# First block's attention as one chain of 16 heads, woven with sections and output projection; modulation and context products placed elsewhere

## The reference

```python
for i in range(DEPTH):                        # 2 layers
    h = rms_norm(x, ln_attn_g[i])
    dq, dk, dv, mq, mk, mv = jnp.split(h @ w_in[i], cuts, axis=-1)   # six sections of 512 columns
    y_diff = diff_attention(...)              # 8 score maps in 4 pairs, a = p0 - lam * p1, value width 128, rms_norm
    y_moba = moba_attention(...)              # 8 heads of 64, causal, 256 keys
    x = x + jnp.concatenate([y_diff, y_moba], axis=-1) @ w_out[i]
    x = x + conv_ffn(rms_norm(x, ln_ffn_g[i]), w_up[i], conv_w[i], conv_b[i], w_down[i])
```

## Time and profile before

| | us |
|---|---|
| median of 3 runs | 2213.57 (2211.42 to 2217.89) |
| the profiled execution: time | 2213.08 |
| its span, first to last instruction | 2211.3 |
| PE busy | 2112.7 (96%) |
| DVE busy | 1361.5 (62%) |
| ACT busy | 961.3 (43%) |
| POOL busy | 206.2 (9%) |

### The profile page before, as it was taken

One profiled execution on the slowest core, in us unless ns is written; L12 is line 12 of the kernel. 1 busy time (PEld: TensorE's weight loads), 2 busy tenths in 40 slices (PEclk: granted clock), 3 DMA queues, 4 the chain that ended last, 5 costly groups with the idle time before them and its releaser, 6 DMA issues.

```text
span 2211.3 us, 31532 instructions
## 1 busy us (share of the span) xinstructions
PE 2112.7 (96%) x12146; PEld 1816.3 (82%) x12146; DVE 1361.5 (62%) x2350; ACT 961.3 (43%) x1602; POOL 206.2 (9%) x173
## 2 busy tenths in 40 slices
PE   7889999989999999998999999999999999999998
PEld 5668998767999888887888778888877899888997
DVE  5646676674777525738454554877565578475565
ACT  4444555544555525344332363223244564445443
POOL 1420000141000100000010000111011000100100
PEclk9979999988999999999999999999999999999999
DMA  9434655522555422212132103534324234251543
GB/s 249 143 123 173 240 182 177 195 95 73 185 191 182 160 100 77 70 57 67 58 105 90 63 20 103 214 132 145 105 89 155 86 115 135 98 178 58 187 157 124
DMA packets 79068, 285.01 MB, mean 129 GB/s; under 512 B 8823, under 2 KB 9731, under 8 KB 78921
## 3 DMA queue, kind: packets, MB, share of 16 engines
q1 hardware_dynamic: 70560, 256.15, 34.4%
q10 hardware_dynamic: 6072, 18.73, 2.3%
q0 software_dynamic: 2288, 8.13, 1.4%
HBM read 277.14 MB, written 5.83 MB: 128 GB/s over the span
## 4 chain that ended last, share of the span: by engine, by line
PE 69%; DVE 8%; ACT 4%; issue 2%; POOL 0%; DVEq 0%; ACTq 0%
PE pb L923 13%; PE pb L925 13%; PE pb L924 13%; PE pb L935 5%; PE pb L937 5%; PE pb L936 5%; PE pb L941 2%; PE pb L1154 2%; PE pb L1257 2%; PE pb L1238 1%; DVE SPL L1916 1%; ACT SPH L1378 1%; PE pb L1082 1%; PE pb L1081 1%; PE pb L1080 1%
## 5 line engine op out<-in xcount | busy, mean ns | idle before, releaser
L1916 DVE TENSOR_TENSOR SPL<-RAW,SPH 128x1024 fp32r<-128x1024 f32 x433 | 524.2, 1229 | 412.9 <-ACT SPH L1378 397.4
L923 PE MATMUL pb<-HTH,SPH 128*128 128x256 f32 (+1 forms) x2008 | 649.8, 324 | 7.9 <-POOL HTL L2518 2.8
L925 PE MATMUL pb<-HTH,SPL 128*128 128x256 f32 (+1 forms) x2008 | 639.7, 319 | 0.0
L924 PE MATMUL pb<-HTL,SPH 128*128 128x256 f32 (+1 forms) x2008 | 639.5, 318 | 0.0
L1378 ACT ACTIVATE SPH<-RAW 128x1024 fp32r<-128x1024 f32 x462 | 475.0, 1047 | 272.6 <-PE pb L925 118.6
L923 PEld LDWEIGHTS pb<-HTH,SPH 128*128 128x128 f32 x2008 | 384.2, 191 | 41.0 <-issue 6.5
L924 PEld LDWEIGHTS pb<-HTL,SPH 128*128 128x128 f32 x2008 | 384.6, 192 | 26.2
L925 PEld LDWEIGHTS pb<-HTH,SPL 128*128 128x128 f32 x2008 | 384.3, 191 | 26.2
L935 PE MATMUL pb<-SPH,HTH 128*128 128x512 f32 x544 | 219.1, 403 | 16.8 <-DVE SPL L1916 6.3
L936 PE MATMUL pb<-SPH,HTL 128*128 128x512 f32 x544 | 214.9, 395 | 0.0
L937 PE MATMUL pb<-SPL,HTH 128*128 128x512 f32 x544 | 214.7, 395 | 0.0
(11 more groups left out here) (275 smaller groups left out, 2827.4 us busy)
## 6 DMA issues: line engine op xcount, KB each, us to landing
RAW<-in_w_up SPq DMA_DIRECT2D x88, 512.0 KB, 4.5
RAW<-in_wa SPq DMA_DIRECT2D x64, 512.0 KB, 3.2
RAW<-in_w_in SPq DMA_DIRECT2D x48, 512.0 KB, 4.6
RAW<-in_wmg SPq DMA_DIRECT2D x48, 512.0 KB, 3.3
RAW<-in_wbr SPq DMA_DIRECT2D x48, 512.0 KB, 3.3
RAW<-in_w_down SPq DMA_DIRECT2D x44, 512.0 KB, 4.5
RAW<-in_w_ada SPq DMA_DIRECT2D x24, 512.0 KB, 4.1
ARAW<-in_w_ada ACTq DMA_DIRECT2D x24, 512.0 KB, 4.3
```

The costliest lines, as they stand in the source:

```text
L923: T.matmul(o, wh[:, kt, :], xh[:, kt, n0:n1], start=kt == 0, stop=False)
L924: T.matmul(o, wh[:, kt, :], xl[:, kt, n0:n1], start=False, stop=False)
L925: m = T.matmul(o, wl[:, kt, :], xh[:, kt, n0:n1], start=False, stop=kt == 7)
L1916: W.tensor_tensor(lo, raw, hi.bitcast(F32), SUB).then_inc(*dve.tick(s["lo_dve"], ("u", u)))
```

## The change

In both layers of the first block the attention is one pipeline of 16 units. Eight twelfths of a step per block are asked for beside the 12 blocks of sections 3 to 5 (the fourth argument of `weave`, 99, keeps the rest of the chain open); the rest is placed by hand between the eight blocks of the output projection, both column groups of which go on together, each block after its `y_turn`. Two modulation groups move from layer 0's attention to its feed-forward part (three groups, one step per tile at tiles 1 to 18). The eight context products move to sections 0 to 2 of layer 1, one after each of the last eight blocks. No low part is made by POOL any more in these stages. `RQ`, `GA` and `SPLIT_ON` go.

```diff
-RQ = ((.8, .7, 2), (.8, 1, 3))
-GA = [2, 1]
-SPLIT_ON = ((0,), (1,))
...
-        side = self.qkv(l, (0, 1, 2), ALL8)
-        next(side), next(side)
-        if l == 1:
-            self.add("stats", "c0")
-        drain(side)
+        rows = self.qkv(l, (0, 1, 2), ALL8)
+        context = self.products("c0", ALL8) if l else iter(())
+        for n, _ in enumerate(rows):
+            if n == 1 and l:
+                self.add("stats", "c0")
+            elif n >= 4:
+                next(context, None)
+        drain(context)
         if l == 0:
             self.add("mask")
         self.add("mark", f"attn{l}")
-        self.split_on[:] = SPLIT_ON[1]
-        weave(self.qkv(l, (3, 4, 5), LO4), self.attn1(l, range(8)), RQ[l][0])
-        first = self.group_n(("wo", l, 0), f"w_out{l}", 0, (0, 1), (0, 1), ("Y", l))
-        self.ada_ring = (3,)
-        extra = self.fill(GA[l]) if l == 0 else self.products("c0", (3,))
-
-        def beside():
-            for _ in range(RQ[l][2]):
-                next(extra, None)
-                yield
-            yield from self.y_turn(l, (0, 1), (2,))
-            next(first)
-            yield
-            next(first)
-            yield
-            yield from extra
-        weave(beside(), self.attn1(l, range(8, 16)), RQ[l][1])
-        self.split_on[:] = SPLIT_ON[0]
-        drain(self.y_turn(l, (2, 3), HI4))
-        drain(first)
-        for g in range(2):
-            if g:
-                drain(self.group_n(("wo", l, 1), f"w_out{l}", 1, (0, 1), (2, 3), ("Y", l), True, 4 + PF))
-            for t in range(2):
-                self.add("res1", l, g, t)
-                self.give(("wo", l, g, t))
+        heads = self.attn1(l, range(16))
+        weave(self.qkv(l, (3, 4, 5), LO4), heads, 8 / 12, 99)
+        out = [self.group_n(("wo", l, g), f"w_out{l}", g, (0, 1), (2 * g, 2 * g + 1), ("Y", l)) for g in range(2)]
+
+        def turn(k2):
+            n = self.take(HI4 if k2 > 1 else (4, 5), ("yT", l, k2))
+            self.add("y_turn", l, k2)
+            self.give(n)
+        for k2, after in ((0, (1, 3)), (1, (2, 2)), (2, (0, 0)), (3, (0, 0))):
+            if k2 == 2:
+                drain(heads)
+            turn(k2)
+            for g in range(2):
+                next(out[g])
+                for _ in range(after[g]):
+                    next(heads)
+                if k2 == 3:
+                    drain(out[g])
+                    for t in range(2):
+                        self.add("res1", l, g, t)
+                        self.give(("wo", l, g, t))
...
-            if l == 0 and 1 <= j < 7:
+            if l == 0 and 1 <= j < 19:
                 next(self.ada)
```

## The result

The change made the kernel slower: 2233.82 us (median of 4 runs, 2232.59 to 2236.68) against 2212.49 for the kernel before on the same chip, a ratio of 1.0096 with a 95% interval of 1.0081 to 1.0111, or 21.3 us. The forecast was 2214, no change that can be told, with 2231 as the upper end; the forecast missed, and the time lies just outside its range.

A forecast was written before the change was run, and what follows sets the result against it. PE bounds the kernel, plus its waits for DVE and ACT and its clock. Layer 0 at -0.4 and layer 1 at +1.2 gave +0.8 us, so 2214 us, no change that can be told; range 2202 to 2231.

The forecast's parts named there:

- the sum for a layer's attention: First scores to last output projection matmul: PE's work, waits, slow clock and small waits add to 104 us per layer.
- Waits, 17.1 and 1 for small ones: PE's idle time in each layer's attention stretch: 17.1 us of named waits, plus 1 us for small waits not seen.
- The walk: Following the new attention order instruction by instruction to find where PE waits for DVE and ACT; 17.1 us per layer.
- Clock, three episodes of 1.8: Nine half-clock matmuls after each of y_turn 0, y_turn 1 and the tail, 5.4 us per layer.
- Work, 80.3: PE's own work in each attention stretch: blocks, scores, transposes and values, 80.3 us, the same for both layers.
- the paragraph on layer 1 before: Same sum for layer 1's old attention left 11 to 12 us, assigned to slow clock; the change gives back half.
- Low parts, cost nothing: Moving 29 low parts from POOL to DVE adds about 8 us of DVE load per layer, costed at nothing.
- Modulation, +7.9: Two modulation groups moved into layer 0's PE-bound feed-forward part cost 4.0 us each there, +7.9 us.
- Context products, +6.4 and +1: Eight products in layer 1's sections 0 to 2 cost 0.8 us each, +6.4, plus 1 for a QKT copy wait.
- Seven steps beside 12 blocks, not eight: Floating-point adding of 8/12 lets only units 0 to 6 go out beside the blocks of sections 3 to 5.
- The clock falls at y_turn 0 and stays down until y_turn 1 is through: Slower rival in both layers' attention: some 8 us more per layer, 2230 us; chance 0.18.
- DVE is late: Slower rival: queued splits make PE wait at each of six section ends, +11 us, 2225 us; chance 0.15.

The follow-up runs named there:

- second: Kernel before, with only the 29 low parts of the attention stages made by DVE and not POOL; 2213.15 us, ratio 1.0010.
- third: Changed kernel, with low parts back on POOL from section 3 to the end of the heads; 2236.54 us, ratio 1.0106.
- fourth: Changed kernel, with layer 1's eight context products moved from sections 0 to 2 to stand two behind each y_turn; 2220.41 us, ratio 1.0041.
- eighth: Changed kernel, reordered behind block 12: a head step or block behind each y_turn, a block ahead of y_turn 1; 2202.93 us, ratio 0.9966.
- first experiment: Kernel before, old attention order, with both modulation groups and the eight context products at their new places; 2213.77 us, ratio 1.0006.
- ninth: Kernel before, with only layer 0's two modulation groups moved from its attention into the first feed-forward part; 2210.65 us, ratio 0.9993.
- fifth experiment: Changed kernel with 0.67 in place of 8/12, so eight head steps go out beside the 12 blocks; 2236.58 us, ratio 1.0112.
- sixth: Changed kernel, with the second block of y_turn 0 placed just ahead of y_turn 1; 2226.27 us, ratio 1.0075.
- seventh: Changed kernel, with y_turn 2 before the last two head steps and y_turn 3 one block earlier; 2224.25 us, ratio 1.0051.

## Why the prediction was wrong

**The step that failed** is the sum for a layer's attention, "80.3 + 17.1 + 5.4 + 1 = 103.8, say 104 us per layer". It measured 114.0 and 117.8 (the table's stretches end one instruction, 0.3 us, later than the prediction's), so 23 to 24 too little for both, which is the whole miss. By its terms:

- *Waits, 17.1 and 1 for small ones:* 21.2 and 24.6. The walk itself was right where it named a wait: y_turn 0 "about 2" (2.07, and 3.48 in layer 1), behind the y_turns 1.5 four times (1.50 to 1.66, four times in both layers), y_turn 1 "about 4.8" (4.40, twice). It missed the QKT copy at 2.88 instead of 1.7, 1.10 for PT, a tail of 2.1 instead of 1 (0.42, 0.42 and 1.27), and in layer 1 another 2.50 for probabilities. Two of these come from changes to which the prediction gave no wait: the QKT copy is awaited longer when DVE makes the low parts (second and third experiments), and the 2.50 comes with the context products in sections 0 to 2 (fourth).
- *Clock, three episodes of 1.8:* four in layer 0 and three in layer 1, but of 7 to 13 block matmuls each; 8.1 and 7.4 us. The prediction tied an episode to "a wait of that size", 4.18 us, and took nine matmuls for it. That rule is what failed: three of the seven episodes began among the heads' small matmuls, before the wait (at 134.1, 519.8 and 550.5), and waits of one size were followed by seven slow matmuls (2.88 at 96.63) or by none (2.88 at 483.38).
- *Work, 80.3:* without the slow block matmuls 84.7 and 85.8 are busy. The eighth, at clock 0.95, still has 83.5 (87.2 less 3.7). So up to some 3 of the difference is work that I priced too low, the eight groups of four transposes and the head steps by one cheap row each, and the rest is small matmuls at the slow clock; no row parts the two.

**The check that should have caught it** is the paragraph on layer 1 before: "11 to 12 left over, which the window with clock 0.58 holds", hence "it gives back half of the slow clock and takes more waits". Nothing was given back: mean clock 0.88 in both layers before, 0.88 and 0.87 after. Part of the left-over was the work that I had under-priced, and I spent it as a gain. The first experiment gives the right comparison, fillers out and order kept, 101.4 and 105.8; against that the forecast of 104 already was no gain, and what was measured is a loss of some 12 in each layer (8 to 13 in layer 0, with the ninth's trace).

**Low parts, cost nothing:** right for the sum (second and third experiments), but not as a mechanism: the move lengthened the wait for the QKT copy and shortened others. **Modulation, +7.9:** right, +7.4. **Context products, +6.4 and +1:** 8.7; PE's busy time 5.8, the rest a wait of 2.53 for a low part on DVE and 0.3 for the QKT copy. With the 2.0 us that they cost later in the chain the price is near 11. "No wait" for the splits was wrong, and +1 for a bank stood in for part of it by chance. **Seven steps beside 12 blocks, not eight:** right, but the fifth experiment shows no gain from an eighth.

**The rivals.** "The clock falls at y_turn 0 and stays down until y_turn 1 is through" (2230) came nearest in time, and as a mechanism half right: the clock was down at y_turn 0 and at y_turn 1 in both layers, but full in between (granted clock 1.00 from 123.9 to 134.1). "DVE is late" (2225) was true in layer 1 for some 5 us (2.53 and 2.50). I gave them 0.18 and 0.15 as if one excluded the other; both happened in part. The range ended at the dearer of them alone.

The Trainium skill ("TensorE: Matmul & The Clock Gate", "What's actually happening") gives the clock two states, 1.2 and 2.4 GHz, and says that the same kernel can show different numbers of slow matmuls in different runs. The traces here agree: block matmuls come 0.23 or 0.43 us apart, and layer 0's attention, with the same instructions in after and in the fourth experiment, had seven slow matmuls behind the wait of 2.88 at 96.63 in one trace and none behind 2.87 at 95.44 in the other.

**Open:** what makes the clock fall. It fell among small matmuls with short waits between them as well as at the longer waits, and no experiment changed one without the other; so how the 10 us of busy time that the eighth saved divide between covered waits and other causes is not shown. Open too is why waits ahead of block 12 differ between traces of the same instructions there: the QKT copy was awaited in layer 1 for 2.88, 1.31, 2.68 and 2.55 (after, sixth, seventh, eighth), y_turn 0 for 3.48, 3.50, 2.05 and 2.05.

## What to carry to other kernels

Where a chain of dependent steps (values, norm, transposes, copy, low part) runs on three engines beside dense matmuls, the place of each block counts more than the mixture: the same instructions took 232 us in one order and 199 in another. Put independent work directly ahead of the consumer of every step that another engine must finish, a head step behind each turn and a block ahead of the next. The side matters: a head step ahead of the turn put its own ACT work in front of the turn's copy, and the wait grew to 6.18 (fifth experiment). And price an order against the old order with the fillers taken out, not against the stretch as it was. Look at the granted clock by itself, and for the moment at which it falls: slow block matmuls behind a wait cost here up to 2.7 us, but in three of seven cases the clock had fallen before the wait began. And follow moved work past its own stretch: the context products cost 8.7 us where they went and 2 more in the next stretch.

## What the runs showed of the hardware that was not expected

The clock fell with no long wait before it: in layer 1 of after it had been full since 533.5, the waits after that were 0.42, 0.42 and 1.27, and at 550.5 it fell. One wait of 2.88 in layer 0 (96.63) was followed by seven matmuls at half clock, the same wait in layer 1 (483.38) by none. A stretch with eight products more in it was 5.2 us shorter (fourth experiment), though 3.3 of that lies in waits that the covers do not explain.

Before the change four of the eight steps of modulation products in layer 0's attention ran wholly or mostly at half clock. Timeline of PE of the kernel before, two steps together at full clock, then two of the four slow ones:

```profile
120.40 1.07 PE L981 MATMUL pb<-RAW,CSP 128*32 128x256 f32 x16
...
150.42 1.08 PE L981 MATMUL pb<-RAW,CSP 128*32 128x256 f32 x8
...
155.01 1.08 PE L981 MATMUL pb<-RAW,CSP 128*32 128x256 f32 x8
```

In the feed-forward part of the kernel after, eight such matmuls take 0.64:

```profile
210.68 0.64 PE L976 MATMUL pb<-RAW,CSP 128*32 128x256 f32 x8
```
